# Weight sums of the first up pair formed in the merge stage and kept in DRAM; two granules exchanged

## What is computed

```python
h = _rmsnorm(x, norm1[l])
proj = jnp.einsum('bsd,de->bse', h, w_in[l])
...
merged = (g[:, :, 0] * jnp.einsum('bsp,pd->bsd', a, w_pool_out[l])
          + g[:, :, 1] * jnp.einsum('bsp,pd->bsd', bconv, w_conv_out[l])
          + g[:, :, 2] * jnp.einsum('bsp,pd->bsd', c, w_attn_out[l]))
x = x + jnp.einsum('bsd,de->bse', merged, w_o[l])
h2 = _rmsnorm(x, norm2[l])
f = jnp.square(jax.nn.relu(jnp.einsum('bsd,df->bsf', h2, w_ff1[l])))
x = x + jnp.einsum('bsf,fd->bsd', f, w_ff2[l])
```

## Time and profile before

| | |
|---|---|
| median of three | 2665.7 us |
| profiled execution, its own time | 2663.93 us |
| its span | 2661.8 us |
| PE busy | 2629.5 us (99%) |
| DVE busy | 2016.8 us (76%) |
| ACT busy | 1242.2 us (47%) |
| DMA, mean | 209 GB/s |
| granted clock of PE, mean | 0.999 |

### The profile page before, as it was taken

The page is one execution under the profiler, slowest core; times in us unless marked ns, Lnnn a source line. Parts: engine busy times, 40 slices in busy tenths (PEclk is TensorE's granted clock), DMA queues, the critical chain, the costliest instruction groups (busy, mean ns, idle before and its releaser), DMA issues.

```text
span 2661.8 us, 36209 instructions
## 1 busy us (share of the span) xinstructions
PE 2629.5 (99%) x14130; PEld 2258.7 (85%) x14130; DVE 2016.8 (76%) x2407; ACT 1242.2 (47%) x1614; POOL 65.3 (2%) x108
## 2 busy tenths in 40 slices
PE   8999999999999999999998999999999999999999
PEld 6688777777888888888888999999998788888887
DVE  4587756657777776577679888888886988888887
ACT  6322343335444453234556656656655433333333
POOL 0000000000000000000000000000001000010000
PEclk9999999999999999999999999999999999999999
DMA  7488765437455557556753566565568777685753
GB/s 246 135 277 291 252 238 182 158 107 243 164 180 182 165 169 265 178 172 213 256 190 129 187 216 197 175 222 182 191 222 323 252 248 275 214 315 169 271 199 121
DMA packets 315940, 557.11 MB, mean 209 GB/s; under 512 B 19648, under 2 KB 126784, under 8 KB 315264
## 3 DMA queue, kind: packets, MB, share of 16 engines
q1 hardware_dynamic: 285936, 456.19, 51.3%
q0 software_dynamic: 22144, 83.89, 8.6%
q10 hardware_dynamic: 7696, 14.81, 1.5%
HBM read 437.25 MB, written 117.44 MB: 208 GB/s over the span
## 4 chain that ended last, share of the span: by engine, by line
PE 87%; DMA 5%; DVE 5%; issue 1%; SPq 1%; ACT 1%; POOL 0%; DVEq 0%; ACTq 0%
PE aux L1203 8%; PE aux L1205 8%; PE aux L1204 8%; PE main L1307 8%; PE main L1309 8%; PE main L1308 8%; PE main L1203 6%; PE main L1205 6%; PE main L1204 6%; PE main L512 3%; PE main L514 3%; PE main L513 3%; DMA t_dram<-stage 1%; DMA stage<-w_o 1%; PE main L1238 1%
## 5 line engine op out<-in xcount | busy, mean ns | idle before, releaser
L1307 PE MATMUL main<-sf,f_wh 128*128 128x256 f32 x1728 | 489.2, 283 | 3.1 <-DVE cf_low L2745 1.7
L1309 PE MATMUL main<-sf,f_wl 128*128 128x256 f32 x1728 | 489.0, 283 | 0.0
L1308 PE MATMUL main<-sf,f_wh 128*128 128x256 f32 x1728 | 489.0, 283 | 0.0
L1307 PEld LDWEIGHTS main<-sf,f_wh 128*128 128x128 f32 x1728 | 331.8, 192 | 3.5 <-DVE cf_low L2745 1.9
L1308 PEld LDWEIGHTS main<-sf,f_wh 128*128 128x128 f32 x1728 | 331.8, 192 | 0.0
L1309 PEld LDWEIGHTS main<-sf,f_wl 128*128 128x128 f32 x1728 | 331.8, 192 | 0.0
L480 ACT ACTIVATE w_hi<-w_raw 128x512 fp32r<-128x512 f32 (+1 forms) x184 | 113.3, 617 | 279.6 <-PE main L514 211.8
L512 PE MATMUL main<-act_hi,w_hi 128*128 128x512 f32 x576 | 229.4, 398 | 8.1 <-DVE w_lo L487 7.2
L1475 ACT ACTIVATE f_wh<-group 128x1024 fp32r<-128x1024 f32 x128 | 135.7, 1061 | 208.4 <-PE aux L1205 107.7
L514 PE MATMUL main<-act_hi,w_lo 128*128 128x512 f32 x576 | 225.4, 391 | 0.0
L513 PE MATMUL main<-act_lo,w_hi 128*128 128x512 f32 x576 | 225.1, 391 | 0.0
(11 more groups left out here) (304 smaller groups left out, 5931.2 us busy)
## 6 DMA issues: line engine op xcount, KB each, us to landing
group<-w_ff SPq DMA_DIRECT2D x160, 512.0 KB, 5.1
f1raw<-w_ff SPq DMA_DIRECT2D x128, 512.0 KB, 5.8
sf<-f_dram POOLq DMA_DIRECT2D x56, 1024.0 KB, 9.3
group_g<-w_in SPq DMA_DIRECT2D x100, 512.0 KB, 4.5
w_raw<-w_in SPq DMA_DIRECT2D x87, 512.0 KB, 4.6
f_dram<-piece_hi SPq DMA_DIRECT2D x112, 256.0 KB, 4.0
f_dram<-piece_lo SPq DMA_DIRECT2D x112, 256.0 KB, 5.2
t_dram<-stage POOLq DMA_DIRECT2D x48, 512.0 KB, 4.5
```

The lines of the kernel that those rows point to most:

```text
L1307: pe.matmul(part, hi_at(8, k)[:, cols], sh, start=first, stop=False, skip_group_check=True)
L1308: pe.matmul(part, hi_at(8, k)[:, cols], sl, start=False, stop=False, skip_group_check=True)
L1309: mm = pe.matmul(part, lo_at(8, k)[:, cols], sh, start=False, stop=last, skip_group_check=True)
```

## The change

The sums of the first up pair (q = 0) leave the pair. Two more staging sets, 12 and 13, load four blocks of w_ff1 each in the merge, behind the loads of its units 8 and 24; DVE makes their sums behind the low halves of units 12 to 15 of chunks 0 and 1 (four sums each), and POOL stores them. In the pair, SP loads t0, t2, t1, t3 from `t_dram` into `f1x` and `f1raw`; b12 of this pair isn't loaded any more. t1 goes over b11 in `f1raw` 0 once that has been split. The third and fourth granule are exchanged, so that b22 comes before t1. The loads for the second pair are issued one by one as buffers come free. POOL's sf loads for the first down sweep have two new conditions: operand 2 waits for a group tile, operands 5 and 6 wait for ten granules of the sweep and not four.

```diff
         stage = [[at(f"stage{h}_{i}", [P, 2, S], F32, o * KB) for i, o in enumerate(at_kb)]
-                 for h, at_kb in enumerate(((66, 133, 137, 154), (72, 76, 104, 108)))]
+                 for h, at_kb in enumerate(((66, 133, 137, 154), (72, 76, 104, 108), (16, 20, 24, 28)))]
...
-        t_dram = nc.dram_tensor("t_dram", (3, 4, 4, P, 2 * S), F32, kind="Internal").ap()
+        t_dram = nc.dram_tensor("t_dram", (4, 4, 4, P, 2 * S), F32, kind="Internal").ap()
...
-            return (16 * (J - 1) if J < 8 else 208 + 16 * (J - 8)) + SUMS.index((i, g)) + 1
+            return (16 * (J - 1) if J < 8 else 200 + 16 * (J - 8)) + SUMS.index((i, g)) + 1
...
-        FIRST_PAIR = ((0, 0), (1, 0), (2, 0), (3, 0), (4, 0), (0, 1), (5, 0), (5, 1), (4, 1), (1, 1),
+        FIRST_PAIR = ((0, 0), (1, 0), (3, 0), (2, 0), (4, 0), (0, 1), (5, 0), (5, 1), (4, 1), (1, 1),
...
-                J, g, h = (0, 6, 7)[s // 4], s % 4, s // 8
-                w, c0 = (w_in, c_gate) if J == 0 else (w_o, (J - 6) * S)
+                J, g, h = (0, 6, 7, None)[s // 4], s % 4, s // 8
+                w, c0 = (w_in, c_gate) if J == 0 else (w_o, (J - 6) * S if s < 12 else 0)
...
+                if s == 12:
+                    sp.wait_ge(g_done, 28 * 6)
+                for b in range(4 if s >= 12 else 0):
+                    r0, col = (b // 2) * (D // 2) + 4 * (s - 12) * P, b % 2 * (D // 2)
+                    sp.dma_start(stage[2][b].rearrange("p a (b c) -> p (a b) c", b=2),
+                                 w_f1[r0:r0 + 4 * P, col:col + COLS].rearrange("(k p) c -> p k c", p=P)
+                                 ).then_inc(stage_landed, 16)
+                for b in range(4 if s < 12 else 0):
                     r0, col = (b // 2) * (D // 2) + 2 * g * P, c0 + b % 2 * (D // 2)
...
+                if g in (u_b + 8, u_b + 24):
+                    load_stage(12 + (g - u_b) // 16)
...
+            def load_t(i, dest, h, landed):
+                sp.dma_start(dest[:, h], t_dram[3, i, h].rearrange("p (k c) -> p k c", k=4)).then_inc(landed[h], 16)
...
+            sp.wait_ge(stage_stored, 64 * 14)
             for h in range(2):
-                for kk, nn in ((0, 0), (0, 1), (1, 1)):
-                    load_f1(0, kk, nn, h)
+                load_f1(0, 0, 0, h)
+                load_f1(0, 1, 1, h)
+                sp.wait_ge(f_lo, 28 * 7 + 24)
+                load_t(0, f1x, h, f1_landed[1])
+                load_t(2, f1raw[1], h, f1_landed[1])
             sp.wait_ge(y_added, 16)
             spill_x2(1, 1)
             sp.wait_ge(f_lo, 28 * 8)
             load_f1(0, 1, 0, 0)
             load_f1(0, 1, 0, 1)
+            sp.wait_ge(f_lo, k_at(0, 0, 0) + 1)
+            load_t(1, f1raw[0], 0, f1_landed[0])
             sp.wait_ge(y_added, 18)
             spill_x2(1, 0)
...
+            sp.wait_ge(f_lo, k_at(0, 1, 0) + 1)
+            load_t(3, f1x, 0, f1_landed[2])
+            for n, h in FIRST_PAIR[2:12]:
+                sp.wait_ge(f_lo, k_at(0, n, h) + 1)
+                if (n, h) == (0, 1):
+                    load_t(1, f1raw[0], 1, f1_landed[0])
+                elif n == 1:
+                    load_t(3, f1x, 1, f1_landed[2])
+                else:
+                    load_f1(1, *{2: (0, 0), 3: (1, 1), 4: (0, 1), 5: (1, 0)}[n], h)
+
+            for q in range(1, F1_PAIRS - 1):
+                spills = [7 * (q - 1) + idx for idx in range(7)]
...
                     act.wait_ge(g_done, 28 * 6)
+                    act.wait_ge(stage_stored, 64 * 14)
...
+                elif q == 0:
+                    j, count = {0: (0, 1), 1: (1, 2), 2: (0, 2), 4: (1, 2), 5: (2, 2 - h), 6: (2, 2 + h)}[n]
+                    act.wait_ge(f1_landed[j][h], 16 * count)
...
             hi1(0, 0, 0)
             hi1(0, 1, 0)
+            hi1(0, 3, 0)
             hi1(0, 2, 0)
-            hi1(0, 3, 0)
...
+                if ci < 2 and 9 <= kt < 13:
+                    mix_stage(12 + ci, kt - 9)
...
-            mix1(0, 0, 0)
             lo1(0, 0, 0)
             lo1(0, 1, 0)
             add_w(7, 7)
             add_w(7, 8)
-            mix1(0, 1, 0)
+            lo1(0, 3, 0)
             lo1(0, 2, 0)
-            mix1(0, 2, 0)
-            lo1(0, 3, 0)
             lo1(0, 4, 0)
             lo_h2(0, 1)
-            mix1(0, 0, 1)
             lo_h2(6, 1)
             lo1(0, 0, 1)
             lo_h2(5, 1)
             lo1(0, 5, 0)
             mix_h2(1, 1)
             lo1(0, 5, 1)
-            mix1(0, 2, 1)
             mix_h2(4, 1)
             lo_h2(4, 1)
             lo1(0, 4, 1)
             lo_h2(1, 1)
             lo1(0, 1, 1)
             mix_h2(2, 1)
-            mix1(0, 1, 1)
             lo_h2(2, 1)
             lo1(0, 2, 1)
             mix_h2(3, 1)
-            mix1(0, 3, 0)
             lo_h2(3, 1)
             lo1(0, 3, 1)
-            mix1(0, 3, 1)
             dve.wait_ge(g_done, k_at(0, 2, 1) + 1)
             dve.wait_ge(kept, 2)
             dve.wait_ge(h2_lo, 14)
...
-            for s in range(12):
-                g, h = s % 4, s // 8
+            for s in range(14):
+                g, h = s % 4, stage_of(s)
...
             for n in (0, 1, 3, 4, 2):
+                if n == 2:
+                    G = G_BASE[8] + 2
+                    pool.wait_ge(group_landed[G % 3], 32 * (G // 3 + 1))
                 load_s(0, n, 28 * 8 + 14 * (F1_PAIRS - 1) + 2 * n + 2)
             for n in (5, 6):
-                load_s(0, n, K2 + 4)
+                load_s(0, n, K2 + 10)
```

More of the change, by code:

```diff
@@ L305, in build, with stage_of @@
         K2 = 28 * 8 + 14 * F1_PAIRS
+        def stage_of(s):
+            return 0 if s < 8 else 1 if s < 12 else 2
         def order_of(J):
@@ L376, in t_at @@
         def t_at(q, i, h):
-            return 80 + 8 * q + (2 * i + h if q else FIRST_SUMS.index((i, h))) + 1
+            return 80 + 8 * (q - 1) + 2 * i + h + 1
         def gs_at(n, h):
@@ L612, in load_stage @@
                     sp.wait_ge(topk_done, 1)
-                for b in range(4):
+                if s == 12:
[6 more added lines that the diff above has]
+                for b in range(4 if s < 12 else 0):
                     r0, col = (b // 2) * (D // 2) + 2 * g * P, c0 + b % 2 * (D // 2)
@@ L849, in load_x2 @@
                              ).then_inc(x2_in, 16)
-            for q in range(F1_PAIRS - 1):
-                spills = [7 * (q - 1) + idx for idx in range(7)] if q else []
+            sp.wait_ge(f_lo, k_at(0, 1, 0) + 1)
[10 more added lines that the diff above has]
+                spills = [7 * (q - 1) + idx for idx in range(7)]
                 def spill_next():
@@ L1009, in _ @@
                 g, q, kt = u_v + n, n // KT, n % KT
-                m = n - SQ_AT
+                m = n - SQ_AT - 1
                 if 1 <= m <= 16:
@@ L1736, in f1_source @@
             def f1_source(q, n, h):
-                return (f1raw[0][:, h], f1x[:, h], f1x[:, h], f1raw[3][:, h], f1raw[1][:, h],
+                return (f1raw[0][:, h], f1x[:, h], f1x[:, h] if q else f1raw[0][:, h], f1raw[3][:, h], f1raw[1][:, h],
                         f1raw[2][:, h], f1x[:, h])[n]
@@ L2002, in mix_stage @@
             def mix_stage(s, i):
-                b11, b12, b21, b22 = [block[:] for block in stage[s // 8]]
+                b11, b12, b21, b22 = [block[:] for block in stage[stage_of(s)]]
                 if i == 0:
@@ L2165, in mix_t1 @@
                     dve.wait_ge(f_lo, K2)
-                    dve.wait_ge(t_done, 208)
+                    dve.wait_ge(t_done, 200)
                 else:
@@ L2596, in mix1 @@
                 if i == 0:
[L2597 to L2600, removed]
+                    dve.wait_ge(f_lo, k_at(q - 1, 6, h) + 1)
+                    dve.wait_ge(f1_landed[0][h], 16 * (q + 2))
+                    dve.wait_ge(f1_landed[1][h], 16 * (q + 2))
                     ins = dve.tensor_tensor(x1, b12, b11, ALU.subtract)
@@ L2612, in mix1 @@
                     dve.wait_ge(t_done, t_at(q, 1, h))
-                    dve.wait_ge(f1_landed[2][h], 16 * (q + 1))
+                    dve.wait_ge(f1_landed[2][h], 16 * (q + 2))
                     ins = dve.tensor_tensor(x1, b21, x1, ALU.subtract)
```

9 lines of the change are left out of this document (4 added, 5 removed).

## The result

The changed kernel takes 2670.47 us (median of 20 runs, 2666.39 to 2673.96), the kernel before 2662.73 us (20 runs, 2658.16 to 2666.44): ratio 1.0028, 95% interval 1.0022 to 1.0034. By the ratio it is slower by 7.5 us. The forecast was 2667.0, which is 2.0 us above the 2665.0 that it took for before. The time lies in the stated range (2661.0 to 2671.5), but the distance is beyond 0.2%, on the side that had a chance of 0.14.

What follows compares the result with a forecast made beforehand. TensorE, busy 99% of the span, was taken as the bound, so only its idle places count. Terms -2.3 + 0.2 + 4.3 + 1.7 - 1.9 = +2.0 us on 2665.0 gave 2667.0 us, range 2661.0 to 2671.5.

Steps and rivals of the forecast that it cites:

- First pair, -2.3: First up pair: with eight sums off DVE, PE's first two waits shrink by 1.1 us each, together -2.3 us.
- the two loop waits: First up pair: later PE waits on a loop through DVE and ACT, which keeps its 3.55 us; gain 0.
- Merge, +4.3: Merge: four copies ahead of the b_raw load of units 10 and 11 make PE wait for low halves, +4.3 us.
- The slow stretch, +1.7: Merge: behind PE's stall of about 2.5 us the clock runs at 1.2 instead of 2.4 GHz, +1.7 us.
- The second set: Merge: second set of stage copies, behind unit 24's load; its delay stays within the 4.9 us in hand, cost 0.
- Start of the pair, +0.2: Start of the first up pair: x_dram spill lands 2.5 us later behind eight copies, eating the slack; +0.2 us, bounds 0 and 2.0.
- the slack of 2.3: Start of the first up pair: time in hand between PE's low half and PE's start at 1386.38, 2.3 us.
- Down sweep, -1.9: First down sweep: with the last two operands' loads held back, a group lands some 3 us sooner; -1.9 us with PE's refill.
- The yb wait: First down sweep: PE's 1.8 us wait for DVE's add to yb, forecast to go.
- the 3.4 us wait: First down sweep: PE's wait for a low half, from a late group tile; forecast to stay.
- The passed-over line, 0: Query and key sweep: PE's sums of squares ask for their operand one unit later; the prediction did not price it.
- The slower rival: Merge: second set of copies holds SP's queue, DVE's product blocks unit 23's low half; 3 plus 1.7 us, 2671.7; chance 0.11.

Runs made afterwards that it cites:

- one_load_later: The changed kernel with each set of stage copies issued one b_raw load later in the merge and summed two units later; 1.0004 of the kernel before, +1.1 us.
- early_spill: The changed kernel with the x_dram spill issued in front of the copies of the first up pair's second half; 1.0013 of the kernel before, +3.5 us.
- before_pool: The kernel before with only the change's two edits on GpSimd's queue (operand 2's wait, operands 5 and 6 after ten granules); 1.0008 of before, +2.1 us.
- before_sq: The kernel before with one line of the change alone: PE's sums of squares wait for sq_low of the unit before; 0.9993 of before, -1.9 us.
- late_stage: The changed kernel with its eight stage copies and sums later in the merge, behind the loads of units 18 and 32; 1.0003 of the kernel before, +0.8 us.

## Why the prediction was right and wrong

The signs of the merge and of the pair, and the mechanism of both, were right. Two terms were wrong, and a third was missing. That the time fell into the range is in part luck: the range was set around 2665.0, 2.3 us above the median of 20, and the same range around 2662.7 would have ended at 2669.2, below the measured 2670.47.

- **First pair, -2.3.** Right: 7.1 - 4.4 = 2.7. The first wait went, the second fell from 1.43 to 0.31, and the two loop waits stayed at 0.90 and 1.82 (the earlier trace rows and the fence above). Only cf_low, 0.3 shorter, was not foreseen.
- **Merge, +4.3.** Right: +4.1 by the table; the load landed at 1072.8 for a forecast of 1073.5, PE's second start is 1079.63 for 1080.4. one_load_later shows the cause. The slow stretch, +1.7, did not come in this execution and came in that of early_spill. In the timed runs it probably comes often: the two kernels without these waits have a mean clock of 0.9985 and 0.9987 against 0.9979, 1.6 to 2.1 us by the estimate above. No run shows it execution by execution, so the term stood better at a chance than at a value. The second set cost nothing, as forecast.
- **Start of the pair, +0.2.** Failed at "the eighth [copy] by 1377.5, and the spill by 1380, 2.5 us later". The program is 3.6 us later here (+3.6 in the table), so that step says 1381.1 and 1383.6. The eighth copy landed at 1382.5, the spill at 1385.4. That is 1.8 beyond the forecast (0.4 of it a slip in the sum: five copies of 1.52 us behind 1370.3 end at 1377.9, not 1377.5), and 4.4 later than in a before shifted by 3.6, which eats the slack of 2.3 and leaves 2.1. That is the upper bound that I had given (2.0), where I took the low end. On top comes a stretch at 1.2 GHz, 0.28 x 6 = 1.7 us, for which I had no term: I expected a stall of 0.2 us, and had seen the clock stay at 1.00 behind 1.8 us of idle. early_spill shows 4 us for the two together, with some 3 of uncertainty.
- **Down sweep, -1.9.** Failed, and its sign with it. The step is "four 1 MB loads now meet the groups after 2074; they are needed near 2101, and land near 2094". It asks when the held loads land, not what lands late because of them. Their victims were SP's group loads and, behind these, its piece stores, which ACT waits for (14.0 us instead of 4.7), and PE lost 2.70 us and a slow stretch. The yb wait fell by 0.9, not by 1.8, and the 3.4 us wait stayed, as forecast. In the table this part is +2.1, in before_pool +2.1 us with 2.4 to either side; I had -1.9. The rule of the Trainium skill that the prediction weighed (DMA: Bandwidth & Descriptors, Queues, rings and completion order: an engine takes turns between queue rows packet by packet) agrees with these rows: SP's small store takes 14.0 us while GpSimd's loads are in flight and 4.7 us when they are not. I applied it to the groups alone.
- **The passed-over line, 0 instead of about -2.** It removed about 2.3 us in the trace and 1.9 in the times of before_sq, so without it the change would stand near +9, by an estimate from these two.
- **Base.** I added to 2665.0, a mean of four; the median of 20 is 2662.7. So the forecast missed the time by 3.5 us, but the distance to before by 5.5.

The sum, from the table and the windows: start of the program +1.4 (chance, before anything that the change touches), sums of squares -2.3, small waits near 610 us +0.3, merge +4.1, up to the pair +2.1, pair -2.7 and its slow stretch +1.7, down sweep +2.1: +6.7. Against the forecast's terms that is +1.9 and +1.7 at the pair's start, +4.0 in the down sweep and +1.4 by chance, less 2.3 for the line passed over, 1.7 for the stretch that did not come in the merge and some tenths: 4.7 in all. The slower rival (the second set holds SP's queue) was not what happened: its sum 2671.7 is near the time for other reasons.

## What to carry to other kernels

Before a transfer is put into a queue, take the loads that will stand behind it one by one and ask which has no time in hand: here a set of copies cost 4.1 us in front of one load and nothing one place further back. When a load is held back, ask what it will meet when it does go, small stores of other queues included, and spread large ones rather than release them together. Read every line of a diff for the wait that it touches, the one-character ones too.

## What the runs showed of the hardware

A stall of PE between 1.81 and 4.27 us is followed by a stretch at 1.2 GHz only sometimes, and its length alone does not decide. Of the stalls of 1.90 us and more (start of the program left out) in the 14 profiled executions, 14 had such a stretch behind them and 10 had not. Without one stood 3.43, 2.89, 2.84, 2.73, five from 2.32 to 2.36, and 2.00; with one stood 1.90, 1.96, 2.07, 2.36, 2.38, eight from 2.70 to 3.58, and 4.27. Length shifts the odds: above 3 us six of 7 had one, from 1.90 to 2.89 eight of 17, and of the 14 stalls of 1.81 or 1.82 us one. A stretch costs 1.7 us (a granted clock of 0.72 over 6 us; the 4 us window of the earlier trace rows caught 1.5 of it), and once, behind 3.16 us in late_stage, twice that (0.62 over 9 us). A forecast should price a stall of 2 to 3 us with about half of 1.7 us, and a longer one with most of it, and a difference of one stretch between two executions says nothing of the kernels.
